# Latent attention's heads on one Trainium2 core: Squares on ScalarE, gains folded into tables and copies, an earlier first query projection, and two modulation pieces loaded one stage sooner

## The reference

```python
def heads_q(cq):
    b, n = cq.shape[:2]
    q = (rmsnorm(cq, q_norm_g) @ w_q_up).reshape(b, n, MLA_HEADS, MLA_QK)
    return rmsnorm(q, q_head_g)

def heads_kv(ckv, kr):
    b, n = ckv.shape[:2]
    kv = (rmsnorm(ckv, kv_norm_g) @ w_kv_up).reshape(b, n, MLA_HEADS, MLA_NOPE + MLA_V)
    k_rope = jnp.broadcast_to(kr[:, :, None, :], (b, n, MLA_HEADS, MLA_ROPE))
    k = rmsnorm(jnp.concatenate([kv[..., :MLA_NOPE], k_rope], axis=-1), k_head_g)
    return k, kv[..., MLA_NOPE:]
```

## Time and profile before

| what | before |
|---|---|
| median of 3 runs | 1547.27 us |
| lowest and highest | 1544.8 and 1548.12 us |
| the profiled execution | 1551.23 us, its span 1549.4 us |
| PE busy | 1279.3 us (83%) |
| DVE busy | 600.3 us (39%) |
| ACT busy | 391.7 us (25%) |
| mean granted PE clock | 0.932 |
| HBM traffic over the span | 327 GB/s |

### The profile page before, as it was taken

How to read it: one execution, slowest core, us unless ns; L and a number is a source line. 1 busy time by engine, 2 the same in 40 slices (tenths; PEclk the granted TensorE clock), 3 DMA queues, 4 the chain that set the end, 5 groups by cost and what they waited for, 6 DMA issues and landing times. The chain is left out here.

```text
span 1549.4 us, 36831 instructions
## 1 busy us (share of the span) xinstructions
PE 1279.3 (83%) x15012; PEld 726.6 (47%) x15013; DVE 600.3 (39%) x1633; ACT 391.7 (25%) x822; POOL 34.0 (2%) x76
## 2 busy tenths in 40 slices
PE   4999989988999997768864899899898996765766
PEld 3445556544565554434432547644454552332333
DVE  2457674427222221211110567765544342212212
ACT  2173343222222322221211322643211211101101
POOL 0102020000000000000001100000000000000000
PEclk9999999999999999988987899999899998888888
DMA  9602988449999999999997630074799999999997
GB/s 358 247 32 83 361 297 327 164 184 386 379 393 426 429 429 428 430 429 429 429 429 302 229 109 0 1 320 162 303 428 426 428 428 428 428 428 428 428 428 327
DMA packets 82716, 507.66 MB, mean 328 GB/s; under 512 B 12965, under 2 KB 17378, under 8 KB 56018
## 3 DMA queue, kind: packets, MB, share of 16 engines
q1 hardware_dynamic: 76152, 489.21, 76.9%
q10 hardware_dynamic: 3306, 8.78, 1.5%
q0 software_dynamic: 3184, 8.63, 1.4%
HBM read 494.58 MB, written 12.01 MB: 327 GB/s over the span
## 5 line engine op out<-in xcount | busy, mean ns | idle before, releaser
L1727 PE MATMUL bank<-sb_ring,sb_scratch 128*32 128x256 f32 x2240 | 138.7, 402 | 52.0 <-DMA sb_ring<-in_moe_w_up 42.4
L1948 PE MATMUL bank<-sb_ring,sb_scratch 128*32 128x256 f32 x1664 | 116.6, 443 | 63.5 <-DMA sb_ring<-in_moe_w_up 58.6
L1813 DVE TENSOR_TENSOR sb_scratch<-sb_scratch,bank 128x128 f32<-128x128 f32 x50 | 14.4, 288 | 318.7 <-ACT sb_scratch L1766 318.7
L1727 PEld LDWEIGHTS bank<-sb_ring,sb_scratch 128*32 128x32 f32 x2240 | 77.4, 116 | 110.6 <-DMA sb_ring<-in_moe_w_up 40.2
L1948 PEld LDWEIGHTS bank<-sb_ring,sb_scratch 128*32 128x32 f32 x1664 | 61.1, 127 | 117.9 <-DMA sb_ring<-in_moe_w_up 58.6
L1770 ACT ACTIVATE sb_scratch<-bank 32x256 f32<-32x256 f32 x200 | 75.0, 375 | 163.2 <-PE bank L1742 161.5
L2033 DVE TENSOR_TENSOR sb_scratch<-sb_scratch,bank 128x128 f32<-128x128 f32 x38 | 10.9, 288 | 242.4 <-ACT sb_scratch L1989 242.4
L1989 ACT ACTIVATE sb_scratch<-bank 128x128 f32<-128x128 f32 x38 | 10.6, 278 | 365.8 <-PE bank L1948 365.8
L1698 PE MATMUL bank<-sb_h,sb_scratch 128*32 128x256 f32 x1632 | 97.9, 379 | 1.5 <-DVE sb_scratch L1800 1.1
L1727 PE MATMUL bank<-sb_scratch 128*32 128x256 f32 x960 | 61.6, 413 | 23.2 <-DMA sb_scratch<-in_moe_w_up 20.5
L1948 PE MATMUL bank<-sb_scratch 128*32 128x256 f32 x768 | 53.7, 442 | 31.2 <-DMA sb_scratch<-in_moe_w_up 29.4
(11 more groups left out here) (413 smaller groups left out, 1906.3 us busy)
## 6 DMA issues: line engine op xcount, KB each, us to landing
sb_ring<-in_moe_w_gate SPq DMA_DIRECT2D x40, 2048.0 KB, 26.6
sb_ring<-in_moe_w_up SPq DMA_DIRECT2D x40, 2048.0 KB, 31.1
sb_ring<-in_moe_w_down SPq DMA_DIRECT2D x39, 2048.0 KB, 33.5
sb_ring<-in_ada_w SPq DMA_DIRECT2D x21, 2048.0 KB, 13.7
sb_scratch<-in_moe_w_gate SPq DMA_DIRECT2D x20, 2048.0 KB, 27.3
sb_scratch<-in_moe_w_up SPq DMA_DIRECT2D x20, 2048.0 KB, 31.4
sb_scratch<-in_moe_w_down SPq DMA_DIRECT2D x20, 2048.0 KB, 33.1
sb_ring<-in_moe_w_gate SPq DMA_DIRECT2D x8, 1024.0 KB, 19.6
```

The source lines that it names most:

```text
L1727: last = nc.tensor.matmul(c.bank(1, 2, FQ)[MB * q:MB * q + MB, :, :], m.xt[:, k, :], m.gu[j][:, :, k, q * FQ:(q + 1) * FQ], start=k == 0, ...
L1813: v.tensor_tensor(m.hm, m.sg, c.ps[1][:, FQ:2 * FQ], ALU.mult).then_inc(hm_ready, 1)
L1948: last = nc.tensor.matmul(c.bank(1, 2, FQ)[MB * q:MB * q + MB, :, :], m.xt[:, k, :], m.gu[j][:, :, k, q * FQ:(q + 1) * FQ], start=k == 0, ...
```

## The change

It touches three places.

In `mla_stage`: the squares of the projected heads are taken by ScalarE out of the banks, ahead of the copies; VectorE only sums them. The head gain is no longer multiplied in on VectorE: ScalarE's copy of the turned heads, which has the head's element on the partitions, scales by a column of it. For tiles that are rotated, the gain of the tail is multiplied into the tables of angles once (`turns`), and that column holds ones for the tail. The shared key tail is not copied to the heads: its sum of squares, from the stage before, is added to each head's, it is rotated once per token, and a multiply writes it to all heads with their factor. The root of the first tile comes ahead of the second tile's copy. `project(0)` comes after the first two query turns, `hold_clock` issues one product instead of three, and the columns of gains are four more small loads, 64 or 96 elements with one to each partition.

In `project_lru_stage`: ScalarE takes the sums of squares of the key latents and tails behind its last four copies, and SP issues modulation pieces 0 and 1, for which the four slots are in another order (piece 0 in the slot that the query latent's weights leave, piece 1 where the first direction's gated inputs were).

In `program`: the slots' order, and the semaphores that now span two stages.

```diff
@@ project_lru_stage
             sp.dma_start(m.wkv, i["mla_w_kv_up"].rearrange("o (k p) n -> p (o k) n", p=P)).then_inc(up_in, 16)
+            sp.wait_ge(product, 8)
+            md.load_weights(sp, 0, ada_in[0])
+            sp.wait_ge(scaled_in, 1)
+            md.load_weights(sp, 1, ada_in[1])
...
-            for u in range(by_vector[-1] + 1, len(units)):
+            for t in range(NT):
+                u = by_vector[-1] + 1 + t
                 copy_out(u)
+                latent, turned = (c.ps[u % NB][:, 0:KVR], c.ps[u % NB][:, KVR:KVR + RP])
+                nc.scalar.activation(m.junk[t][:, 0:KVR], latent, ACT.Square, accum_out=m.kv_sum[:, t:t + 1])
+                nc.scalar.activation(m.junk[t][:, KVR:KVR + RP], turned, ACT.Square, accum_out=m.rope_sum[:, t:t + 1])
...
                 step(v.tensor_tensor(b[:, :, :], b[:, :, :], gi[:, :, :], ALU.mult))
+                if d == 0:
+                    dve.sem_inc(scaled_in, 1)
@@ mla_stage, SP
+            for j, name in enumerate(("mla_q_head_g", "mla_k_head_g")):
+                col = i[name].rearrange("o (f one) -> (o f) one", one=1)
+                sp.dma_start(m.gain_cols[0:NOPE, 2 * j:2 * j + 1], col[0:NOPE]).then_inc(small_in, 16)
+                sp.dma_start(m.gain_cols[0:QK, 2 * j + 1:2 * j + 2], col).then_inc(small_in, 16)
-            for a in range(md.n):
+            for a in range(2, md.n):
...
-            for load, freed in zip(next_chunks, (md.n - 3, md.n - 1, md.n)):
+            for load, freed in zip(next_chunks, (md.n - 3, md.n - 2, md.n)):
@@ mla_stage, PE
             def project(n):
                 t = n % NT
                 if n >= 2:
-                    pe.wait_ge(up_out, n - 1)
+                    pe.wait_ge(up_squared, 2 * (n - 1))
+                    pe.wait_ge(up_out, up_copies(n - 2))
...
+            turn_queries(0)
+            turn_queries(1)
+            c.hold_clock(c.ps[0][:], 1)
+            pe.wait_ge(cq_t, 1)
             project(0)
+            for t in range(2, NT):
+                turn_queries(t)
+            for t in range(NT):
+                turn_latents(t)
+            pe.wait_ge(cq_t, NT)
+            pe.wait_ge(ckv_t, NT)
             project(1)
@@ mla_stage, ScalarE
-            for t in range(NT):
-                c.act_chain.step(nc.scalar.activation(m.junk[:, 0:KVR], m.tm[:, t, QR:QR + KVR], ACT.Square, accum_out=lat[:, t:t + 1]))
-            act.sem_inc(lat_sum, 1)
...
+                for q in range(2):
+                    nc.scalar.activation(squares(n)[:, 4 * q:4 * q + 4, :], parts[q][:, :, 0:width], ACT.Square).then_inc(up_squared, 1)
+                for q in range(2):
+                    nc.scalar.activation(rows[n % 2][:, 4 * q:4 * q + 4, 0:width], parts[q][:, :, 0:width], ACT.Copy).then_inc(up_out, 1)
...
             copy_up(0)
+            root(0)
             copy_up(1)
-            root(0)
...
-                    last = nc.scalar.activation(dst_t[0:QK, 4 * q:4 * q + 4, t * P:(t + 1) * P], c.bank(q, 4, P)[0:QK, :, :], ACT.Copy)
+                    last = nc.scalar.activation(dst_t[0:QK, 4 * q:4 * q + 4, t * P:(t + 1) * P], c.bank(q, 4, P)[0:QK, :, :], ACT.Copy,
+                                                scale=m.gain_cols[0:QK, col:col + 1])
@@ mla_stage, VectorE
+            dve.wait_ge(small_in, 16 * 7)
+            for which, g in enumerate((m.qg, m.kg)):
+                halves = g[:, NOPE:].rearrange("p (a two f) -> p a two f", a=2, two=2)
+                for two in range(2):
+                    by_axis = halves[:, :, two, :].unsqueeze(1).to_broadcast([P, 2 * LT, 2, RP // 4])
+                    go(v.tensor_tensor(m.turns[which][:, two],
+                                       m.rope.rearrange("p c t a f -> p (c t) a f"), by_axis, ALU.mult))
             dve.wait_ge(lat_root, 1)
             step(v.reciprocal(lat, lat))
...
             for n in range(N):
...
+                dve.wait_ge(up_squared, 2 * (n + 1))
+                step(v.tensor_reduce(ss, squares(n), AX.X, ALU.add))
+                if n < NT:
+                    v.tensor_scalar(ss, ss, 1.0 / QK, EPS, ALU.mult, ALU.add).then_inc(mean_r, 1)
+                else:
+                    v.tensor_scalar(ss, ss, m.rope_sum[:, t:t + 1], 1.0 / QK, ALU.add, ALU.mult).then_inc(mean_r, 1)
+                dve.wait_ge(up_out, up_copies(n))
+                dve.wait_ge(root_r, n + 1)
+                step(v.reciprocal(ss, ss))
+                by_head = ss.unsqueeze(2)
+                if n < NT:
+                    step(v.tensor_tensor(w3, w3, by_head.to_broadcast([P, NH, QK]), ALU.mult))
+                    if t < LT:
+                        rotate(w3[:, :, NOPE:], 0, t, n, NH)
+                else:
+                    step(v.tensor_tensor(w3[:, :, 0:NOPE], w3[:, :, 0:NOPE], by_head.to_broadcast([P, NH, NOPE]), ALU.mult))
+                    step(v.tensor_tensor(w3[:, :, NOPE:], m.tm[:, t, QR + KVR:TM].unsqueeze(1).to_broadcast([P, NH, RP]),
+                                         by_head.to_broadcast([P, NH, RP]), ALU.mult))
                 dve.sem_inc(head_ready, 1)
+                if LT <= n < NT:
+                    rotate(m.tm[:, n - LT, QR + KVR:TM].unsqueeze(1), 1, n - LT, n, 1)
@@ program
-        late = Modulation(c, [(0, 4, Modulation.CH), (1, 0, 2)], [(c.ring[0], j * KC * BANK) for j in range(3)] + [(c.ring[1], KC * BANK)],
+        late = Modulation(c, [(0, 4, Modulation.CH), (1, 0, 2)], [(c.ring[1], KC * BANK)] + [(c.ring[0], j * KC * BANK) for j in (1, 0, 2)],
```

More of the change, by code:

```diff
@@ L497, in __init__ @@
         self.rope_flat = c.h_flat[:, o + 2 * QK:o + 2 * QK + 64]
+        self.turns = [cut(c.h_flat, o + 2 * QK + 64 + 128 * j, 2, 2 * LT, 2, RP // 4) for j in range(2)]
+        self.kv_sum, self.rope_sum, self.gain_cols = (c.stat[:, a:a + NT] for a in (4, 16, 20))
         self.lam = c.scr[:, 15264:15272]
@@ L788, in _ @@
         def _(pool):
+            for j in range(2):
+                nc.gpsimd.memset(m.gain_cols[NOPE:QK, 2 * j:2 * j + 1], 1.0).then_inc(gains_set, 1)
+                pool.wait_ge(gains_set, j + 1)
             md.preset_tables(preset)
@@ L802, in _, with turn_latents @@
                 last.then_inc(query_turned, 1)
-                if t == 1:
-                    c.hold_clock(c.ps[0][:], 3)
-            for t in range(NT):
+            def turn_latents(t):
                 pe.wait_ge(lat_norm, t + 1)
@@ L907, in _, with rotate @@
             md.spread_columns(columns)
-            dve.wait_ge(small_in, 48)
+            step(v.tensor_scalar(m.rope_sum, m.rope_sum, QK * EPS, None, ALU.add))
+            def rotate(w, which, t, n, heads):
+                t1, t2 = (m.sq[n % 2][:, j * 128:j * 128 + 16 * heads].rearrange("p (h a f) -> p h a f", h=heads, a=2) for j in range(2))
+                rope_with_gain(c, w, m.turns[which], t, t1, t2, heads, RP // 4)
             for n in range(N):
```

84 lines of the change are left out of this document (41 added, 43 removed).

## The result

The changed kernel has a median of 1536.87 us (8 runs, 1530.74 to 1547.24) beside 1547.30 us for the kernel before on the same chip (8 runs, 1543.24 to 1551.54): a ratio of 0.9938, 95% interval 0.9914 to 0.9963. (A ratio is not exactly the quotient of the two medians.) The forecast was 1538.2 us, 9.1 us less.

A forecast was written before the change was run, and what follows sets the result against it. PE was taken as nearest to the bound in the heads stage, working 63.60 of 73.95 us. Terms -4.5 - 1.7 - 3.1 + 0.2 = -9.1 us took the median from 1547.27 to 1538.2 us, range 1534.5 to 1543.

The forecast's parts named there:

- Step 1: Recurrence stage's end: ScalarE's added Squares behind its last four copies make it end later, +0.9 us.
- Step 2: Heads stage's opening: first projection from 2.2 to 6.2 us, small loads landed at 5.5, second projection ends at 13.6.
- rival of late columns: Opening: gain columns land late; at 12.5 us no visible change, 1546.9 (chance 0.07); at 39.8 slower, 1574 (chance 0.06).
- Step 3: First tile: head turns start at 15.6 us, set by PE with 0.4 to spare; -4.5 us including the later start.
- Step 4: From first to second tile's head turns: 6.77 us instead of 8.45 without the idle time before, -1.7 us.
- rival of a low clock in the opening: Heads stage's opening: first two projections run at the low clock, costing 3.4 us; time 1541.6, chance 0.18.
- Step 5: Later tiles: DVE's shorter chain removes waits of 1.27, 1.17 and 0.68 us, leaving only PE late; -3.1 us.
- Table loads in each tile: Heads stage: Squares and roots need loads, 1.28 us each, 1541.0; second estimate, 2.66 us a switch, 1546.5; chance 0.02.
- Step 6: Heads stage's end: last transposes to the end stay 2.70 us, plus 0.2 for the scale; +0.2 us.
- cover of the modulation loads: Heads stage: two early pieces keep products from waiting; without them some 3 of the 9 us would be lost.
- A low stretch that falls elsewhere: Opening of the stage after the heads: its low-clock stretch moves away, up to 3 us more gain, 1535; chance 0.04.
- later stages move as a whole: Stages after the heads: they start sooner when an earlier stage ends sooner, so its gain reaches the total.

The follow-up runs named there:

- e3: Changed kernel with the first query projection back behind all query turns and three clock-holding products; heads stage 69.83 us, ratio to the kernel before 1.0002.
- e5: Changed kernel with one clock-holding product on PE before each tile's head turns; heads stage 70.42 us.
- e6: Changed kernel with one more 0.96 us multiply on DVE before each tile is ready; heads stage 65.14 us.
- e2: Changed kernel without the two early modulation pieces, all ten loaded in the heads stage; stage 69.86 us, ratio to the kernel before 0.9966.
- e9: Changed kernel once more, unedited; median 1539.68 us, ratio to the kernel before 0.9965, heads stage 63.04 us.
- e7: Changed kernel with the key latents normed before DVE waits for the small loads; heads stage 62.93 us, ratio to the kernel before 0.9958.
- e8: Changed kernel with one clock-holding product before each of attention's first four turns; median 1538.09 us, ratio to the kernel before 0.9957.
- e10: Changed kernel with holding products before attention's first four turns, run again; median 1538.76 us, ratio to the kernel before 0.9948, heads stage 63.06 us.
- e11: Changed kernel with latents normed before the small-load wait and holding products in attention; median 1540.99 us, ratio to the kernel before 0.9965.
- e12: Changed kernel with one or two holding products before each tile's turns, 12 in all; heads stage 73.85 us, ratio to the kernel before 0.9998.
- e4: Kernel before with the first projection moved up, one holding product and two early pieces, old DVE and ScalarE work; heads stage 76.78 us, ratio 1.0012.
- e1: Kernel before with only modulation pieces 0 and 1 loaded early, slots in new order; heads stage 73.75 us, ratio 1.0000.

## Why the prediction was right

*Step 1, the stage before.* Forecast +0.9. The work is as described, the cost was put too high. From the last product's end to the next stage's first turn it was 0.75 us (142.25 to 143.00) and is 1.28 (144.96 to 146.24): +0.5. The last copy starts at 144.99 and takes 0.41; the Squares behind it are done at 145.94. From the start of the Square of 256 to that of the 32-wide one it is 0.36 us where I took 0.54, and the 32-wide one with its read is done in 0.28 where I took 0.36. The stage began at 146.15, not 143.8, because the recurrence stage itself started 2.7 us later in this execution, not by this.

*Step 2, the opening.* P0 forecast to start at 2.2, started at 2.0. P1 forecast to end at 13.6, ended at 13.2. The columns landed, in the DMA view:

```profile
sb_stat<-in_mla_k_head_g SPq DMA_DIRECT2D x1, 0.2 KB, 2.2
...
sb_stat<-in_mla_k_head_g SPq DMA_DIRECT2D x1, 0.4 KB, 2.2
```

The bounds were 1.8 and 9.6 us and 2.6 was chosen: well judged between them, but no row had said so. With 64 and 96 elements they land no later than the 32 and 48 KB tables beside them, which took 2.4 to 2.7 us. The Trainium skill ("DMA: Bandwidth & Descriptors", Rules for kernel authors) has such a load go as one descriptor per element; no cost of that shows here. The issues took 0.49 to 0.58 us each, a little more than the 0.42 of the earlier trace rows. The rival of late columns is refuted at both its prices.

*Step 3, the first tile.* T0 forecast 15.6 from the start of the stage, with 0.4 to spare; it came at 15.0 with 0.36 to spare. Right, and set by PE as the prediction had it.

*Step 4.* T0 to T1 forecast 6.77; 6.77 (161.15 to 167.92). It is the size best foretold, taken from a pair of tiles in the same timeline that had no wait. The rival of a low clock in the opening didn't come: P0 and P1 took 4.14 and 4.11 us. e3 shows that it was near: with no P0 in the gap they take 10.42 together, 7.98 before.

*Step 5, the later tiles.* Forecast -3.1 with nothing late but PE: no wait at any turn, and e5 and e6 show which engine is the bound. The room is smaller than step 5 read it: 4.9 us of chain against 5.9 for the tiles with rotation, but PE waited in e6 for 0.46 us at T1 when 1.0 was added. In the changed kernel DVE is ready for T1 5.1 us behind the end of T0 (162.23 to 167.33), and PE is there after 5.7 (167.92): 0.6 us of room. And T7, which has no projection between it and T6, was not looked at on its own: its room is 0.3 us (DVE ends at 206.08, PE starts at 206.39).

*Table loads in each tile.* That rival didn't come: the stage's only load is the one in its opening, where ScalarE's line reads

```profile
146.20 1.28 ACT L888 ACT_TABLE_LOAD   x1 [0.26 <-PEq L560]
```

and the Squares at L902 and the roots at L912 take turns eight times behind it. From that load to the root are 1.30 us (146.20 to 147.50), so a change of set costs half of the 2.66 us in the prediction's second estimate here. The Trainium skill ("ScalarE: Activation LUTs", Table sets: the hidden batching unit) doesn't name Square in the root's set. The trace settles it for this pair: no batching was needed.

*Step 6, the end.* From T7's start to the stage's end 2.70 us became 2.86, forecast +0.2. A copy with a scale column takes 684 ns where the plain one took 593, 91 more. The Trainium skill ("ScalarE: Activation LUTs", What ACT_TABLE_LOAD costs) gives some 93 ns for a pointer operand, and the trace agrees. The cover of the modulation loads is where the prediction was wrong: "some 3 of the 9 us would be lost" without it, 6.8 in e2. The missing part is what it had counted for DVE's waits and not here: a wait at the end is followed by products at the low clock, and the pieces were short at four products, not at the tenth alone.

*A low stretch that falls elsewhere* was the rival for more gain. It didn't come: the opening of attention is 15.67 us in the changed kernel's trace and 15.62 before. It does vary, from 13.3 to 15.7, but from execution to execution, with the old chain as with the new one.

*The sum.* Stage forecast -10.0 (73.95 to 63.95) and -9.1 with step 1; measured -10.8 and -10.3. Of the 1.2 us of excess, 0.6 is in step 3 and 0.4 in step 1. So the prediction is right in sign and mechanism, and within 1.2 us for the stage.

For the whole kernel the agreement is partly luck. The first comparison gave 0.9938, where the forecast is 0.9941. But e9, the same kernel again, gave 0.9965, and the versions whose stage is as long within 0.1 us gave 0.9958 (e7), 0.9957 (e8), 0.9948 (e10) and 0.9965 (e11): all six together say 5 to 10 us. The stage's -10.3 us alone would be 0.9933, and four of the six intervals leave it out (they begin at 0.9934 for e7, 0.9939 for e8 and 0.9942 for e9 and e11). So one claim of the prediction is not quite right: **later stages move as a whole**. Most likely something is given back outside the stage. The output stage's opening gives back some 1.1 us in every trace of the changed program, which leaves -9.2 us or 0.9941, and the intervals of e9 and e11 begin just above that. Whether more is given back stays open: the other stages vary too much from execution to execution, and e12, with the gain padded away, costs nothing that shows (0.9976 to 1.0020).

## What to carry to other kernels

When two engines are nearly level and the weights come in just in time, parts of a change can't be priced one by one: here the new order with the old chain cost 2.9 us, the pieces alone brought 0.1, and all together brought 10.8. For each part ask what stands ahead of it in the queues of the others, and what limit is met next.

Before an idle gap is filled, look at what the gap does to the clock behind it, and in more than one execution. Real work moved into a gap (P0 here) can win twice, the time it took elsewhere and the clock behind the gap. Holding products win the clock alone and cost PE their own time.

Read a local change in its own stage, if that stage repeats from trace to trace (this one does, to 0.1 us; the others don't), and the whole by many runs. A stage's gain is not the kernel's: 10.3 us here, and 5 to 10 in the total.

## What the runs showed of the hardware

- A stretch of PE's waits can cost more than its length. Behind 2.35 us of idle time P0 and P1 took 2.4 us longer (10.42 in e3, 7.98 before), behind 2.45 us P0 took 1.7 longer (5.83 in e4, 4.14 in the changed kernel).
- It isn't the same each time. Behind 3.78 or 3.79 us of idle time before T0, T0 and P2 together took 6.57 us in before, 6.43 in e1 and 7.76 in e4. Behind two waits of 1.18 and 0.96 us, four products of attention took 3.62 us in before and in the changed kernel, 3.11 in e9 and 1.88 in e5.
- The landing of a 128 KB table (in_before) took 2.3 to 2.4 us in the three executions with the old chain and 3.0 to 3.8 in the eleven with the new code. The 1 MB loads issued just ahead of it took longer too, 6.2 to 6.8 us instead of 5.8 to 6.0. The cause is open.
- Four columns of 64 or 96 elements, each element to its own partition, landed 2.2 to 2.3 us after their issue in the changed kernel.
- ScalarE's Square and its root need no table load between them: in the stage they take turns eight times behind one load of 1.28 us.
